# Expert weights of a mixture-of-experts layer: from half matrices to whole matrices per transfer

## What is computed

```
# per token: a group of experts by softmax, then the two best experts in it, with weights
# 32 experts; w_gate, w_up [1024, 512], w_down [512, 1024], all float32
y_e = (silu(x_e @ w_gate[e]) * (x_e @ w_up[e])) @ w_down[e]
x = x + gate2 * sum over the two experts of a token (weight * y_e)
out = rms_norm(x, g_final)
```

## Time and profile before

| | |
|---|---|
| median of three runs | 1805.96 us |
| profiled execution, its own time | 1808.0 us |
| its span | 1806.2 us |
| PE busy | 1687.4 us (93%) |
| mean granted clock of PE | 0.979 |
| DMA, mean over the span | 203 GB/s, 366.34 MB |
| expert loads, 1 MB each | 64 for gate, 64 for up, 64 for down; 27.3, 28.3 and 28.0 us from issue to landing (median) |

### The profile page before, as it was taken

One profiled execution on the slowest core, in us unless ns is written; L12 is line 12 of the kernel. 1 busy time (PEld: TensorE's weight loads), 2 busy tenths in 40 slices (PEclk: granted clock), 3 DMA queues, 4 the chain that ended last, 5 costly groups with the idle time before them and its releaser, 6 DMA issues. The chain is left out here.

```text
span 1806.2 us, 21681 instructions
## 1 busy us (share of the span) xinstructions
PE 1687.4 (93%) x8252; PEld 1156.9 (64%) x8253; DVE 776.3 (43%) x1338; ACT 501.2 (28%) x821; POOL 193.1 (11%) x251
## 2 busy tenths in 40 slices
PE   6999999989999999999999999999999999999982
PEld 4788887766776878878887778777933333333321
DVE  6245224768676687423335455353521111111114
ACT  4313324555323212222224433253210111111101
POOL 1020000000112122200003000001211111110101
PEclk9999999999999999999999999999999999999997
DMA  9423220024444567422221222126889999999995
GB/s 306 115 70 117 94 93 1 1 94 158 174 155 165 201 240 242 157 71 93 93 93 36 91 73 70 47 98 279 328 338 424 423 424 424 425 424 424 425 418 209
DMA packets 114500, 366.34 MB, mean 203 GB/s; under 512 B 21723, under 2 KB 24967, under 8 KB 89807
## 3 DMA queue, kind: packets, MB, share of 16 engines
q1 hardware_dynamic: 108219, 355.45, 52.3%
q0 software_dynamic: 5760, 9.02, 1.3%
q10 hardware_dynamic: 404, 0.30, 0.1%
HBM read 359.85 MB, written 16.84 MB: 209 GB/s over the span
## 5 line engine op out<-in xcount | busy, mean ns | idle before, releaser
L2457 PE MATMUL x_upa<-x_ring,x_Ta 128*64 128x512 f32 x608 | 135.1, 593 | 12.5 <-DMA x_ring<-in_w_expert_up_dram 12.5
L2457 PE MATMUL x_gpa<-x_ring,x_Ta 128*64 128x512 f32 x608 | 135.8, 598 | 4.8 <-DMA x_ring<-in_w_expert_gate_dram 3.1
L2457 PEld LDWEIGHTS x_upa<-x_ring,x_Ta 128*64 128x64 f32 x608 | 46.3, 137 | 98.7 <-issue 98.7
L372 DVE TENSOR_TENSOR p_lo<-p_raw,p_hi 128x2048 fp32r<-128x2048 f32 (+1 forms) x20 | 44.7, 2237 | 140.3 <-ACT p_hi L685 140.3
L2457 PEld LDWEIGHTS x_gpa<-x_ring,x_Ta 128*64 128x64 f32 x608 | 46.0, 138 | 90.9 <-issue 88.7
L379 PE MATMUL fr_p<-p_hi,u_high 128*128 128x512 f32 x224 | 90.0, 402 | 0.0
L381 PE MATMUL fr_p<-p_hi,u_low 128*128 128x512 f32 x224 | 88.7, 396 | 0.0
L380 PE MATMUL fr_p<-p_lo,u_high 128*128 128x512 f32 x224 | 88.7, 396 | 0.0
L2519 ACT ACTIVATE x_siga<-x_gpa 128x512 f32<-128x512 f32 x19 | 11.3, 597 | 241.4 <-PE x_gpa L2457 241.4
L2482 PE MATMUL x_y0a<-x_ring,x_aTa 128*64 128x512 f32 x304 | 72.9, 600 | 5.1 <-ACT x_aTa L2524 4.6
L685 ACT ACTIVATE p_hi<-p_raw 128x2048 fp32r<-128x2048 f32 (+1 forms) x20 | 37.5, 1873 | 129.2 <-DMA p_raw<-in_w_in_dram 129.2
(11 more groups left out here) (885 smaller groups left out, 3943.9 us busy)
## 6 DMA issues: line engine op xcount, KB each, us to landing
x_ring<-in_w_expert_gate_dram SPq DMA_DIRECT2D x64, 1024.0 KB, 27.3
x_ring<-in_w_expert_up_dram SPq DMA_DIRECT2D x64, 1024.0 KB, 28.3
x_ring<-in_w_expert_down_dram SPq DMA_DIRECT2D x64, 1024.0 KB, 28.0
p_raw<-in_w_in_dram SPq DMA_DIRECT2D x18, 1024.0 KB, 5.0
adaw0m<-in_w_ada_dram SPq DMA_DIRECT2D x6, 2048.0 KB, 10.9
adaw1m<-in_w_ada_dram SPq DMA_DIRECT2D x6, 2048.0 KB
ada_first<-in_ada_w_dram SPq DMA_DIRECT2D x8, 1024.0 KB, 5.2
w_raw0m<-in_mlp_w_dram SPq DMA_DIRECT2D x8, 1024.0 KB
```

What stands on the lines that cost most here:

```text
L372: return v.tensor_tensor(out, x, high.bitcast(F32), ALU.subtract)
L2457: mm = nc.tensor.matmul(ps[CAP * f:CAP * f + CAP, :], self.xT[:, k, CAP * f:CAP * f + CAP], w[m + f][k // 4][:, k % 4, :], start=(k == 0), ...
```

## The change

A transfer carries a whole matrix, 2 MB, 16 KB in a row for each partition. A slot holds one matrix and has one semaphore (11 in place of 22). The order in a pair is gate of the first expert, gate of the second, up, up, down, down. PE's waits for a first and a second half are now both for the whole matrix. SP frees a slot when the whole product of the pair's last round that read it is done; the half-way semaphores are still stepped, and nobody waits for them. In `out_route`, slot 5 is loaded whole after step 4 of `W3.low_ready`, slot 7 after `O.used` is 3, and slot 6 whole after `O.ready`.

```
@@ out_route, sync
-                for half in range(2):
-                    sp.wait_ge(W3.low_ready, 3 + half)
-                    ring.load_half(sp, 10 + half)
+                sp.wait_ge(W3.low_ready, 4)
+                ring.load(sp, 5)
                 sp.wait_ge(O.used, 3)
-                ring.load_half(sp, 12)
                 ring.load(sp, 7)
                 sp.wait_ge(O.ready, 2 * NT)
-                ring.load_half(sp, 13)
+                ring.load(sp, 6)
@@ Ring
-        self.landed = s.sems("x_ring_landed", 2 * SLOTS)
+        self.landed = s.sems("x_ring_landed", SLOTS)
     def of(self, q):
-        return [[self.half_slot(self.number(q, m, half)) for half in range(2)] for m in range(6)]
+        return [[self.tiles[(6 * q + m) % SLOTS][:, 4 * half:4 * half + 4, :] for half in range(2)] for m in range(6)]
     def arrived(self, q):
-        return [[(self.landed[c % (2 * SLOTS)], 16 * (c // (2 * SLOTS) + 1))
-                 for c in (self.number(q, m, half) for half in range(2))] for m in range(6)]
+        return [[(self.landed[w % SLOTS], 16 * (w // SLOTS + 1))] * 2 for w in range(6 * q, 6 * q + 6)]
+    def load(self, sp, w, pair=None):
+        q, m = w // 6, w % 6
+        load_expert(sp, self.A, m, (q if pair is None else pair) * 2 + m % 2, self.tiles[w % SLOTS][:, :, :]).then_inc(self.landed[w % SLOTS], 16)
@@ first_places, sync
-                free = [(X.half_read[i], ready) for i, ready in enumerate((X.gate_ready, X.up_ready, X.down_ready))]
+                free = (X.gate_ready, X.up_ready, X.down_ready)
-                    for j in range(12):
-                        c = 12 * q + j
-                        if c + 2 * SLOTS < 12 * PAIRS:
-                            if j in (0, 2):
-                                pair = pair_at(sp, (c + 2 * SLOTS) // 12)
-                            sp.wait_ge(free[j // 4][j % 4 // 2], done)
-                            ring.load_half(sp, c + 2 * SLOTS, pair)
+                    for m in range(6):
+                        w = 6 * q + m
+                        if w + SLOTS < 6 * PAIRS:
+                            if m in (0, 1):
+                                pair = pair_at(sp, (w + SLOTS) // 6)
+                            sp.wait_ge(free[m // 2], done)
+                            ring.load(sp, w + SLOTS, pair)
```

More of the change, by code:

```diff
@@ L2606, in _ @@
                     done = sp.snap(ran)
-                    for j in range(12):
-                        c = 12 * q + j
-                        if c + 2 * SLOTS < 12 * PAIRS:
-                            if j in (0, 2):
-                                pair = pair_at(sp, (c + 2 * SLOTS) // 12)
-                            sp.wait_ge(free[j // 4][j % 4 // 2], done)
-                            ring.load_half(sp, c + 2 * SLOTS, pair)
[L2614 to L2617, removed]
+                    for m in range(6):
[5 more added lines that the diff above has]
+                            ring.load(sp, w + SLOTS, pair)
+                        elif w % SLOTS == PARKED:
+                            sp.wait_ge(free[m // 2], done)
+                            sp.dma_start(h[:, :, :], h_dram.rearrange("(t p) d -> p t d", p=P)).then_inc(h_back, 16)
                 sp.wait_ge(F.moved, 1)
```

## The result

The changed kernel takes 1812.4 us in the median of 5 runs (1809.46 to 1812.67), the kernel before 1805.86 in 5 runs beside it (1800.74 to 1807.57). The ratio is 1.0035, with an interval of 1.0019 to 1.0052: 6.3 us slower (3.4 to 9.4). That is inside the range of 1802 to 1817 and within the half per cent that I had called "same", 2.4 us above the predicted 1810.0. The profiled execution took 1812.48 us, with a span of 1810.7.

A forecast was written before the change was run, and what follows sets the result against it. The prediction took the DMA weight stream to lead in the last third, plus PE's work after the last landing. 3.4 + 1.0 - 5.0 + 3.4 + 1.2 = +4.0 us gave a median of 1810.0 us, range 1802 to 1817.

The forecast's parts named there:

- Start: Start of the unbroken expert stream: first freed-slot load goes out after the whole first gate product, not half; +3.4 us.
- Filling the ring: Slots filled before the experts: slot 6 loads whole and late, so the first gather lands later; +1.0 us (0 to 2.5).
- Gathers in the stream: Gathers beside the weight stream: even at 14.3 us to landing, 5 us of cover stay; costed at nothing.
- Rate: Weight stream after the first freed load: 16 KB packets halve the packet count and its cost; -5.0 us (-7.7 to 0).
- End: Last pair: all 32 down matmuls, not 16, stand behind the last landing; +3.4 us.
- Up adds nothing: Last pair: the up product would let down start 0.5 us before down's weights land, so no extra cost at full clock.
- Clock at the end: Last pair: PE's longer wait for up lowers its clock to half speed for a while; +1.2 us (0 to 2.9).
- Issues: SP's list: 96 loads in place of 192, but SP waits for landings and slots, not its own issue time; 0.
- B: Rival, weight stream: packets stay at 8 KB, so nothing is refunded; 9.0 us slower, 1816 us; chance 0.21.
- C: Rival: full 7.7 us packet refund, and the end costs only the down product; -0.9 us, 1805 us; chance 0.14.
- D: Rival: later slot releases starve the stream near its start and at the double rounds; +10.8 us, 1817 us; chance 0.06.
- E: Rival, weight stream: each transfer carries a fixed time, which half the transfers halve; 1796 us; chance 0.04.

The follow-up runs named there:

- e1: Kernel before, half transfers and half waits kept, but a half slot is freed only when the whole product is done: 1808.07 us, ratio 1.0014.
- e6: Changed kernel, but slots 8, 9 and 10 are first filled with two 1 MB transfers each: 1808.68 us, ratio 1.0019.
- e2: Changed kernel, but each matrix goes as two 1 MB transfers on its one semaphore, with one wait for both: 1810.72 us, ratio 1.0032.
- e5: Changed kernel, but only the last pair's two down matrices go as halves in the old order: 1809.52 us, ratio 1.0035.
- e3: Changed kernel, but the first two loads into freed slots go in halves, each sent as its half is read: 1808.01 us, ratio 1.0014.
- e4: Changed kernel, but the last two pairs' matrices go as halves in the old order, with a wait for each half: 1807.29 us, ratio 1.0012.
- e7: Changed kernel, but halves for slots 6 to 10 at the fill, the first two freed loads and the last two pairs: 1802.57 us, ratio 0.9994.
- e8: e7, but 512 KB quarters for the first two freed loads and the last two down matrices: 1803.41 us, ratio 0.9999.

## Why the prediction was right, and where it was off

- *Start, +3.4.* Right in the trace (8.74 against 5.35; 3.5 in e1 at the full clock). What it left out is that the stream behind the earlier, half start ran 0.9 to 1.0 longer, so the late one costs 2.5 net. Later releases cost nothing, as costed: e1 has them all late, and its whole sum is explained by the first.
- *Filling the ring, +1.0 (0 to 2.5).* Too small: with the transposes behind it the term measured +3.1, above its range. The step was right in kind, the gather is the one that is late, but I had sized it by the extra 1 MB of slot 6 and gave the longer packets "a little". From the ring's first load to the transpose it is +2.3, with the gather's issue no later than before in that frame (73.1 to 73.3 us after the first load in both), so it lies in the gather's own flight: 10.3 us instead of 7.8, of which up to 1.0 can be the later filling (e6), for which I had 0.7. The transposes then took 1.09 instead of 0.68, after 2.99 us of standing, at the low clock (+0.8 by the gate product). The Trainium skill (DMA: Bandwidth & Descriptors, Queues, rings and completion order) says that an engine takes turns between queues packet by packet. In the stream the trace agrees in direction: a gather lands in 11.1 us against 8.8. But what it takes over a free one (3.3 and 3.4 us) went from 5.5 to 7.7 and did not double.
- *Gathers in the stream, nothing.* Right: 10.0 to 12.4 us, median 11.1, under the 14.3 that I had allowed.
- *Rate, -5.0 (-7.7 to 0).* The mechanism was right, packets of 16 KB, and the size was off: 452.3 (e1, e2) to 449.2 (changed) is -3.1. 765 packets less on each engine are then 4.1 ns each, not 6.5: I had taken 65% of the records' 10.1 ns as real, it was 40%. The mean rates say the same, 427 against 424 GB/s, 0.7% of 450 us.
- *End, +3.4 for down.* Right to the tenth: 7.09 - 3.65. "Up adds nothing, 0.5 before down's landing" was right as well, and e5 shows what it implied: with up whole, halves of down alone win 0.5.
- *Clock at the end, +1.2 (0 to 2.9).* Wrong, it was 0. The dip came, and as long as the upper end had it: the gate product took 9.96 instead of 7.1 after 3.29 us of standing, granted clock 0.52 in this window:

```profile
1752.40:1758.40 6.00, 6.00 (x16) 1.95 (x18) 0.00 (x0) 0.00 (x0) 0.19 (x1) 0.52 1.00 424
```

It fell on gate, which waited for up's landing anyway (0.42 us of idle were left), and not on up, where I had put it. In e2, e3, e5 and e6 the same product took 8.4 to 8.8 us after 3.3 us of standing, and up's wait swallowed it there too.

- *Issues, 0.* Right; see the last section.

The sum, then: 3.4 - 4.0 + 3.4 + 2.3 + 0.8 = +5.9 by the trace, in which the -4.0 are the packets' 3.1 and the 0.9 of the half start. Predicted was +4.0. The refund was 1.9 too large and the fill with its transposes 2.1 too small; the clock's 1.2, which did not come, hid part of this, and so did the 0.9 of the half start. The total was nearer than its terms, and that part is luck.

Do the timings bear the fill's term out? For each kernel I take what start, stream and end make of it by its trace (with the start at the full clock, 1.8 for a quarter, 3.65 for a half and 7.1 for a product; where no DMA releases down, all from the first freed load to PE's end), and what was timed beyond that:

| kernel | by start, stream, end | timed | left over |
|---|---|---|---|
| changed | +2.8 | +6.3 | 3.5 |
| e3 | +0.4 | +2.5 | 2.1 |
| e4 | -0.1 | +2.2 | 2.3 |
| e5 | +2.3 | +6.3 | 4.0 |
| e1 (8 KB at the fill) | +2.5 | +2.5 | 0.0 |
| e2 (8 KB) | +5.9 | +5.8 | -0.1 |
| e6 (8 KB in three slots) | +3.0 | +3.4 | 0.4 |
| e7 (8 KB) | -2.9 | -1.1 | 1.8 |
| e8 (8 KB) | -3.4 | -0.2 | 3.2 |

With 16 KB packets beside the first gather 3.0 are left over in the mean, with 8 KB 1.1. That is the 2 us of the gather, in direction and size, and e2 and e6, which fill slot 6 late but with 8 KB, have nothing left over, which speaks for the packets and against the later filling. But every row is uncertain by 2 to 3 us and e8 does not fit: it points to the fill and doesn't prove it. What takes the gain that the traces of e7 and e8 show is open.

The rivals: B (packets stay at 8 KB) is refuted by the page's count. C (full refund, nothing at the fill) is refuted in both: the refund is 3.1 (e2) and not 7.7, and the first transpose was 2.3 late; that the end costs only the down product was right (e4). D (the stream starves) had one clear place: a window at 0.90 and 379 GB/s from 1656 to 1662, after the last double round, with which I had said I would be wrong. The window of the earlier trace rows, 1640 to 1670, runs at 416 GB/s because of it, against 424 before. SP had issued nothing from 1628.60 to 1661.25, so some engines had run dry, while others still worked on earlier loads until 1673.21. It cost nothing that I can find: e2 has the same hole (0.92 and 384 GB/s from 1657.65 to 1663.65) and e1 has none, and both streams are 452.3. The statement was too strict, as a share below 1.00 is not yet a later end. E (a fixed time for each transfer) is refuted: half the transfers gave 0.7%. The 2 us for a transfer that the prediction took from the Trainium skill (DMA: Bandwidth & Descriptors, Anatomy of one DMA) are stated there for transfers that GpSimd issues, not for SP's; in SP's full queue no run here shows them.

## What to carry to other kernels

When a full queue feeds an engine, larger transfers give only the packets' cost back, here 0.7% of the stream, and the grain of waiting and freeing costs one share of a product at each end of the stream, 2.5 and 3.4 us here, whatever the transfers' size. So if transfers are coarse, let it be in the middle, with fine ones at both ends: e7 beats whole matrices throughout, though it isn't shown to beat halves throughout, and still finer ones (e8) gave nothing. At the end look for the second chain before refining only the last transfer. And the small transfers beside the longer packets landed later, 11.1 us instead of 8.8, which matters only where one of them is waited for.

## What the hardware did that I had not expected

The queue's limit did not go by bytes. Landing times of the expert loads issued from 1417 to 1434 us, changed kernel, and SP's longest kind of wait (total, times, longest):

```profile
DMA to landing us min/median/max: 43.6/44.3/48.7
```
```profile
SPq L2283 <- PE x_gpa L2442: 158.1, 15, 36.4
```

Before, SP's issues themselves took 2 us each in the full stream, with about 11 transfers of 1 MB in flight (28.4 us to landing in the median). Now most take 0.33 to 0.36 (the longest 2.3), although about 9 transfers of 2 MB are in flight, more bytes than before, and SP waits for PE, as the ring has only 11 slots. So the bytes in flight were not what held SP's issues before; that it is the number of transfers fits, but what sets the limit the runs don't show.

The 16 engines don't end together: in the kernel before the DMA share fell from 1.00 at 1756 to 0.44 at 1766 to 1768, while the last matrix, for which PE waited, landed only at 1771.5. So some engines had nothing left while others were still at work. Why they differ is open, and also why a stream begun by a half product loses 0.9.
